# Splitting the last columns ahead of each RMS norm into two token halves in a two-layer trunk kernel

## What is computed

```python
def _rms(x, eps=NORM_EPS):
    xf = x.astype(jnp.float32)
    return (xf * lax.rsqrt(jnp.mean(xf * xf, axis=-1, keepdims=True) + eps)).astype(x.dtype)
def _modulate(h, shift, scale):
    return _rms(h) * (1.0 + scale) + shift
def _swiglu(h, w13, w2):
    a, b = jnp.split(h @ w13, 2, axis=-1)
    return (jax.nn.silu(a) * b) @ w2
for i in range(DEPTH):                       # DEPTH = 2, D = 1024, F = 2816
    h  = h  + 0.5 * ml[2] * _swiglu(_modulate(h,  ml[0], ml[1]), ffn1_w13[i], ffn1_w2[i])
    hc = hc + 0.5 * mc[2] * _swiglu(_modulate(hc, mc[0], mc[1]), ffn1_w13[i], ffn1_w2[i])
    a_l, a_c = _modulate(h, ml[3], ml[4]), _modulate(hc, mc[3], mc[4])
    o_l, o_c = mixer(a_l, a_c)               # i = 0: differential attention, i = 1: retention
    h = h + ml[5] * o_l
    h = h + 0.5 * ml[8] * _swiglu(_modulate(h, ml[6], ml[7]), ffn2_w13[i], ffn2_w2[i])
    # the context stream hc does the same in layer 0 only
return _rms(h) * final_norm_g
```

## The kernel before

| norm | phase ahead of it | phase behind it |
|---|---|---|
| n=1 | down, 16 chunks, 512 tokens | diff_qk, 512 tokens |
| n=2 | down of the attention, 4 chunks of 8, 512 tokens | up, 512 tokens |
| n=3 | down, 16 chunks, 512 tokens | up, 512 tokens |
| n=4 | down, 16 chunks, 512 tokens | ret_q, 256 tokens |
| n=5 | down of the retention, 8 chunks of 8, 256 tokens | up, 256 tokens |

## Time and profile before

### The profile page before, as it was taken

How to read it: one execution, slowest core, us unless ns; L and a number is a source line. 1 busy time by engine, 2 the same in 40 slices (tenths; PEclk the granted TensorE clock), 3 DMA queues, 4 the chain that set the end, 5 groups by cost and what they waited for, 6 DMA issues and landing times.

```text
span 2025.1 us, 28709 instructions
## 1 busy us (share of the span) xinstructions
PE 1951.5 (96%) x10376; PEld 1669.6 (82%) x10376; DVE 1155.0 (57%) x1834; ACT 661.6 (33%) x1020; POOL 203.4 (10%) x248
## 2 busy tenths in 40 slices
PE   8899999989988889999999899999989999999998
PEld 7688888878965678888888788888878998999998
DVE  3877773254368557787532777752352533656554
ACT  2323222232336332222222332222233422544443
POOL 1210100120001230100010310000120000011000
PEclk9799999989989889999999999999979999999999
DMA  7365652324210026656333355533224220455554
GB/s 280 119 204 187 195 173 88 99 85 161 84 63 1 1 68 211 198 188 198 122 92 106 134 198 192 194 119 101 86 86 154 95 83 22 132 181 165 175 166 138
DMA packets 80989, 270.61 MB, mean 134 GB/s; under 512 B 8992, under 2 KB 14368, under 8 KB 80800
## 3 DMA queue, kind: packets, MB, share of 16 engines
q1 hardware_dynamic: 62496, 202.69, 30.5%
q0 software_dynamic: 18432, 67.12, 10.3%
HBM read 268.72 MB, written 1.05 MB: 133 GB/s over the span
## 4 chain that ended last, share of the span: by engine, by line
PE 89%; DVE 7%; issue 2%; ACT 1%; POOL 1%; DMA 0%; DVEq 0%; POOLq 0%; SPq 0%; ACTq 0%
PE pt L1011 24%; PE pt L1012 24%; PE pt L1014 24%; PE pt L1186 2%; PE pt L1187 2%; PE pt L1185 2%; DVE tmp L790 2%; PE pt L1269 1%; DVE wl L643 1%; DVE tmp L784 1%; PE pt L1221 1%; PE pt L1202 1%; PE pt L1042 1%; DVE small L915 1%; PE pt L1259 1%
## 5 line engine op out<-in xcount | busy, mean ns | idle before, releaser
L643 DVE TENSOR_TENSOR wl<-raw,wh 128x1024 fp32r<-128x1024 f32 (+2 forms) x396 | 440.0, 1151 | 570.9 <-ACT wh L462 567.2
L1011 PE MATMUL pt<-xh,wh 128*128 128x512 f32 (+1 forms) x1824 | 662.2, 363 | 16.6 <-ACT xh L518 9.6
L1012 PE MATMUL pt<-xh,wl 128*128 128x512 f32 (+1 forms) x1824 | 659.8, 362 | 0.0
L1014 PE MATMUL pt<-xl,wh 128*128 128x512 f32 (+1 forms) x1824 | 651.8, 363 | 7.8 <-POOL xl L416 7.5
L462 ACT CAST wh<-raw 128x1024 fp32r<-128x1024 f32 (+2 forms) x396 | 365.5, 970 | 271.3 <-PE pt L1014 248.2
L1011 PEld LDWEIGHTS pt<-xh,wh 128*128 128x128 f32 x1824 | 351.5, 193 | 71.2 <-issue 11.0
L1014 PEld LDWEIGHTS pt<-xl,wh 128*128 128x128 f32 x1824 | 347.6, 192 | 65.5 <-POOL xl L416 15.8
L1012 PEld LDWEIGHTS pt<-xh,wl 128*128 128x128 f32 x1824 | 351.5, 193 | 50.6
L656 DVE CUSTOM_DVE_ANT_0 pt<-modw,raw 128x1024 f32<-128x1024 f32 x256 | 305.7, 1256 | 8.4 <-DMA modw<-in_mod_rows 8.3
L1011 PE MATMUL pt<-uh,wh 128*128 128x512 f32 (+1 forms) x704 | 257.5, 366 | 0.3 <-DVE wl L643 0.3
L1012 PE MATMUL pt<-uh,wl 128*128 128x512 f32 (+1 forms) x704 | 257.4, 366 | 0.0
(11 more groups left out here) (144 smaller groups left out, 1671.1 us busy)
## 6 DMA issues: line engine op xcount, KB each, us to landing
raw<-in_ffn_w SPq DMA_DIRECT2D x240, 512.0 KB, 4.0
modw<-in_mod_rows POOLq DMA_DIRECT2D x128, 512.0 KB, 4.0
raw<-in_ret_w_in SPq DMA_DIRECT2D x48, 512.0 KB, 4.3
raw<-in_diff_w_in SPq DMA_DIRECT2D x24, 512.0 KB, 4.2
raw<-in_ffn_w SPq DMA_DIRECT2D x32, 256.0 KB, 3.8
raw<-in_ret_w_out SPq DMA_DIRECT2D x16, 512.0 KB, 4.0
region<-in_mod_start SPq DMA_DIRECT2D x9, 512.0 KB, 8.6
raw<-in_ffn_w SPq DMA_DIRECT2D x32, 128.0 KB, 3.4
```

The source lines that it names most:

```text
L643: nc.vector.tensor_tensor(flat(wl[:, s, cut]), raw[:, raw_slot(late, s, p), 0:part_rows * CW], flat(wh[:, s, cut].bitcast(F32)), ALU.subtr ...
L1011: nc.tensor.matmul(bank, wh[:, s, k, cut], hi(k), start=a, stop=False)
L1012: nc.tensor.matmul(bank, wl[:, s, k, cut], hi(k), start=False, stop=False)
L1014: return nc.tensor.matmul(bank, wh[:, s, k, cut], lo(k), start=False, stop=b)
```

## The change

The last group of down (two output tiles) ahead of norms 1 to 5 is computed for the first half of the tokens and then for the second half, 256 tokens each (128 each at n=5). The first half takes all chunks of the group; the second takes the last two, which are still in wh and wl, and then the first two again (chunks 16 and 17, loaded once more; none at n=2 and n=5). The norm is made half by half: the first half's beside the passes of the second half, the second half's beside the first products of the next phase, which take their first pair of chunks by halves too (first_pair). Casts and rests of the chunks to come are put between tiles of the norm (split_at). The squares of the last two tiles are added on VectorE into ssq (fold), so each half needs two sum matmuls. Waits for weights are by piece (piece), waits for a PSUM bank by tile (claim). `small` gets 192 words, so that uh starts at byte 139136, a multiple of 128; oh and region move with it. The final norm is not split, but uses fold.

```diff
-        small = sb("small", [P, 176])
+        small = sb("small", [P, 192])
+        def chunks(ph):
+            return 4 * len(ph["rows"]) + ph["again"]       # again: 2 for four chunks a group, else 0
+        def last_group(ph):
+            nc_ = len(ph["rows"])
+            at = 3 * nc_
+            kept = range(max(nc_ - 2, 0), nc_)
+            return ([(at + e, e, 0) for e in range(nc_)] + [(at + e, e, 1) for e in kept]
+                    + [(4 * nc_ + e, e, 1) for e in range(ph["again"])])
+        def split_at(ph):
+            return {4: ({0: 16, 3: 17, 6: 18, DT: 19}, DT), 2: ({0: 8, 4: 9}, 2), 1: ({4: 5}, 2)}[len(ph["rows"])]
...
 VectorE, norm
+                    def normed_tile(half, k):
+                        i, cut = half * DT + k, slice(half * H, (half + 1) * H)
+                        if i >= 2:
+                            dve.wait_ge(x_hi_done, ph["xh"] + i - 1)
+                            dve.wait_ge(affine, ph["xh"] + i - 1)
+                        nc.vector.tensor_tensor(tmp[:, k % 2, cut], hT[:, k, cut], pt[:, BC + half, 0:H],
+                                                ALU.mult).then_inc(normed, 1)
+                    def statistics(half):
+                        norm_mean(ph["st"] + half, slice(half * H // P, (half + 1) * H // P), 4 + half)
+                        dve.wait_ge(bcast_ready, ph["st"] + half + 1)
+                    take_half(ph, 0)
+                    statistics(0)
+                    for k in range(DT):
+                        if k in splits:
+                            rest_chunk(ph["before"], splits[k])
+                        if k == other:
+                            take_half(ph, 1)
+                        if k == 0:
+                            normed_tile(0, 0)
+                        if k + 1 < DT:
+                            normed_tile(0, k + 1)
+                        affine_tile(0, k)
+                    if other == DT:
+                        take_half(ph, 1)
+                    if DT in splits:
+                        rest_chunk(ph["before"], splits[DT])
+                    statistics(1)
+                    normed_tile(1, 0)
+                    for k in range(DT):
+                        if k + 1 < DT:
+                            normed_tile(1, k + 1)
+                        affine_tile(1, k)
-                        rest(2 * q0 + 1, 1, late=late)
...
 ScalarE, norm
+                    half_squares(ph, 0)
+                    for k in range(DT):
+                        if k in splits:
+                            split_chunk(ph["before"], splits[k])
+                        if k == other:
+                            half_squares(ph, 1)
+                        half_tile(0, k)
...
 TensorE
+            def piece(chunk, k):
+                for p, row0 in enumerate((0, halves_of(DT)[0])):
+                    if k == row0:
+                        pe.wait_ge(lo_ready, 2 * chunk + p + 1)
+            def first_pair(ph, halves):
+                for half in halves:
+                    cut = slice(half * H, (half + 1) * H)
+                    for s in range(2):
+                        for k in range(DT):
+                            if half == 0:
+                                piece(2 * ph["q"] + s, k)
+                            pe.wait_ge(x_hi_done, norm["xh"] + half * DT + k + 1)
+                            ... (wh and wl by xh, both tiles; wait x_ready; wh by xl, both tiles)
+                            if half == 0 and s == 0 and k == DT // 2 - 1:
+                                half_sums(norm, 1)
+                            if half == 0 and s == 0 and k == DT - 1:
+                                half_spread(norm, 1)
...
 TensorE, down, behind the first three groups
+                        sums_at, spread_at = {4: ((0, 5), (1, 5)), 2: ((0, 7), (1, 7)), 1: ((0, 4), (1, 2))}[nc_]
+                        for i, (m, e, half) in enumerate(passes):
+                            for t in range(2):
+                                if first:
+                                    claim(half, s0[half] + 2 - half, t)
+                                for k in range(ph["rows"][e]):
+                                    if t == 0 and fresh:
+                                        piece(2 * q0 + m, k)
+                                    ... (three matmuls of T // 2 tokens)
+                                    if i == first_end + 1 and (t, k) == sums_at:
+                                        half_sums(norm, 0)
+                                    if i == first_end + 1 and (t, k) == spread_at:
+                                        half_spread(norm, 0)
+                            if spent:
+                                ins.then_inc(chunk_done, 1)
```

More of the change, by code:

```diff
@@ L110, in plan @@
             add("diff_attn", x=DH)
-            add("down", q=2, s=2, L=L, f=0, T=TOK, gate=5, half=1.0, rows=(8,))
+            down(L=L, f=0, T=TOK, rows=(8,), split=True)
         else:
@@ L455, in _, with split_chunk @@
         def _(act):
+            def split_chunk(ph, m):
+                chunk = 2 * ph["q"] + m
+                split(chunk // 2, chunk % 2, rows=chunk_rows(ph, m), late=chunk >= 2 * late_pair)
             def split(pair, s, rows=DT, late=False):
@@ L637, in _, with rest_chunk @@
         def _(dve):
+            def rest_chunk(ph, m):
+                chunk = 2 * ph["q"] + m
+                rest(chunk, chunk % 2, rows=chunk_rows(ph, m), late=chunk >= 2 * late_pair)
             def rest(chunk, s, rows=DT, late=False):
@@ L1004, in _, with products @@
         def _(pe):
-            def products(s, out_set, nk, hi, lo, T, start, stop, between=None, by_row=None):
+            def products(chunk, s, out_set, use, nk, hi, lo, T, start, stop, between=None, by_row=None):
                 def one(t, k, parts):
@@ L1023, in products @@
                     if stop:
[L1024 removed]
+                        a.then_inc(first_tile_done[out_set], 1)
                 else:
@@ new lines, in half_sums @@
+            def half_sums(norm, half, width=None):
+                H = width or norm["T"] // 2
+                pe.wait_ge(unit_step, UNIT_STEPS * (norm["unit"] - START_UNITS))
+                pe.wait_ge(sq_folded, norm["fold"] + 2 * (half + 1))
+                for b in range(H // P):
+                    ins = nc.tensor.matmul(pt[:, 4 + half, b:b + 1], ssq[:, half * H + b * P:half * H + (b + 1) * P], ones[:, 0:1],
+                                           start=True, stop=True)
+                ins.then_inc(sum_ready, 1)
@@ L1113, in norm_spread, with half_spread @@
+            def half_spread(norm, half, width=None):
+                H = width or norm["T"] // 2
+                pe.wait_ge(rstd_ready, norm["st"] + half + 1)
+                for b in range(H // P):
+                    at = half * H // P + b
+                    ins = nc.tensor.matmul(pt[:, BC + half, b * P:(b + 1) * P], rstd[:, at:at + 1].broadcast_to([P, P]), ident,
                                            start=True, stop=True)
@@ new lines, in _ @@
+                    for m in range((3 if ph["split"] else 4) * nc_):
+                        j, e = divmod(m, nc_)
+                        k0, rows_, g = first_row(ph, e), ph["rows"][e], j % 2
+                        by_row = None
+                        h_, l_ = (lambda k, k0=k0: hi(k0 + k)), (lambda k, k0=k0: lo(k0 + k))
+                        if m == 0 and not ph["f"]:
+                            by_row = (lambda k: pe.wait_ge(ready, upto + k + 1), lambda k: None)
+                        elif j == 0:
+                            pe.wait_ge(ready, upto + k0 + rows_)
+                        products(2 * q0 + m, m % 2, g, s0[g] + j // 2, rows_, h_, l_, T, e == 0, e == nc_ - 1, by_row=by_row)
```

483 lines of the change are left out of this document (267 added, 216 removed).

## The result

The changed kernel takes 2046.51 us (median of 4 runs, 2046.38 to 2051.52) beside 2025.31 us for the kernel before on the same chip (4 runs): a ratio of 1.0108, 95% interval 1.0091 to 1.0125. It is slower by 21 us, and outside my range (2023, 1997 to 2038).

What follows compares the result with a forecast made beforehand. TensorE was taken as the bound, busy 96% of the span, with 70.6 us of waits at five norms to win. Norm, address and final-norm terms summed to -3.3 us from 2026.3, giving 2023 us, range 1997 to 2038.

Steps and rivals of the forecast that it cites:

- Norms 1 to 3: Last down group through first pair behind each norm: changes of +0.6, -4.1 and +1.4 us forecast for n=1, 2 and 3.
- The table from S: Step times from S, start of the last down group, to the end of the first pair of chunks behind each norm.
- the rival that weights are not late: At n=1, 3 and 4 most of 11.4 us of stalls each would vanish: 1996 us, or some 1980; chance 0.25.
- Norm 4: Last down group through ret_q's first chunks: -1.1 us, with ret_q's second pair's first rest behind the second half's tiles, S+61.5.
- The address: Aligning u saves 7.0 us over 1188 matmuls at 512 tokens; at 256 tokens u costs +1.5 and o +2.2 us.
- Norm 5, the step that failed: 128-token matmuls at n=5 taken at 0.067 us each: 34.3 us for the stretch against 31.5 before, +2.8 us.
- The rule of the Trainium skill: A weight load of 128 columns takes 107 ns; by it n=5 costs +15.5 us, not +2.8, and the sum is 2035.
- one at 2036 us: Rival: the 384 matmuls of 128 tokens at n=5 are bound by their weight load, +12.7 us; chance 0.18.
- The clock rival: Stops of 2 to 3 us in split groups keep TensorE at 1.2 GHz, 1 to 3 us a norm: 2030 us; chance 0.07.
- The sum: All terms over the norms, the address of u and the final norm together: -3.3 us, giving 2023 us.

Runs made afterwards that it cites:

- experiment 5: Changed kernel with norm 5's down, norm and first pair whole at 256 tokens, loads of chunks 14 to 17 cut to 16 columns: 2004.58 us, ratio 0.9898.
- experiment 10: Matmuls alone, 72 per place of hi, lo and weights; 512 columns took 226.7 ns with hi and lo 0 or 256 bytes off, 228.9 at 64, 232.4 at 128.
- Experiment 2: The kernel before with one edit, small at 192 words so that u starts at a multiple of 128 bytes: 2018.51 us, ratio 0.9966.
- experiment 7: Changed kernel with only norm 5's first pair whole at 256 tokens, its last down group and tiles still in halves: 2030.82 us, ratio 1.0023.

## Why the prediction was wrong

*Norms 1 to 3, right.* The table from S gave 67.1, 42.4 and 67.1 us; measured 67.5, 42.2 and 67.4. Its waits in norm 1 were 2.5, 2.1, 0.8, 2.8, 2.2 and 1.0 us ahead of chunks 14, 15, 17, 18, the second sums and the second spread. Taken from start to start less one matmul they are 2.6, 1.7, 0.5, 2.9, 1.4 and 1.4. The cause of the first three is shown by experiment 5; the wait ahead of chunk 18 was left as it is there. So the rival that weights are not late is out, and the gain of the halves was zero by design: hidden norm out, open weight loads in.

*Norm 4, near.* I gave -1.1 us and it was 0.0. The wait for ret_q's second pair is there (4.4 us ahead of its first chunk at 1500.0, predicted 1501.8), and another 1.3 ahead of its second, which I had left out.

*The address, right in kind.* -7.0 us predicted, 1188 x 0.0066 = -7.8 measured, and +1.5 and +2.2 at 256 tokens came to 528 x 0.0014 = +0.7 and 288 x 0.0052 = +1.5. "Alignment" to 128 bytes was not the right name for it: in experiment 10 a place 128 bytes off is no faster than one 64 off. Experiment 2 shows it alone: 2018.5 of 2026.2 us.

*Norm 5, the step that failed.* "No row excludes either; I take 0.067." The 128-token matmul measured 0.111 us at the high clock, the bound that the earlier trace rows had given. 384 x 0.044 = 16.9 us. The rule of the Trainium skill that I weighed and set aside ("TensorE: Matmul & The Clock Gate", LDWEIGHTS: 107 ns for 128 columns, whatever the width of x) agrees with the 111 that 192 and 128 columns have in common. The row nearest in width said 0.111 and the rule said so too; the line through 512 and 256 tokens was an extrapolation past the point where another limit takes over.

The second part is the clock, which my sum for norm 5 put at nothing. The 144 matmuls at 0.2136 instead of 0.111 cost another 14.8 us. Together 31.7 over my 34.3, less some 2 that lay in the shadow of the paced tiles: 63.8. I had the two as rivals, one at 2036 us and one at 2030, and gave each its chance alone. The clock rival looked for stops in the split groups of 256 tokens. There the clock stayed at 1.00 at norms 1, 2 and 4 and fell once, at norm 3, for 3.4 us:
```profile
1077.03:1080.44 3.41, 3.41 (x19) 3.41 (x18) 0.00 (x0) 1.03 (x2) 0.00 (x0) 0.50 0.52 174
```
Norm 3 took 67.4 us even so, like norm 1. The rival did not look at the pair of norm 5, where the narrow matmuls make the stops matter. That dense narrow matmuls don't bring the clock back no row of before showed; but the range should have held both rivals at once, 2036 + 15 = 2051.

*The sum.* +1.0 - 4.5 + 1.6 + 0.0 + 32.2 - 7.8 + 0.7 + 1.5, and 2.3 us behind norm 5 while the clock recovers (117.5 us for 960 matmuls, 115.2 before), make +27.0; the spans differ by 19.7. The missing 7.3 us are in stretches that the diff doesn't touch: 4.7 ahead of the first u matmul (303.78 before, 299.06 after), 1.7 between norms 1 and 2, and 1.0 between norms 4 and 5. Part of the first is the clock. Before, after, and in experiment 7, whose code is the changed kernel's up to there and whose first u matmul comes at 303.2:
```profile
81.92:88.75 6.83, 5.05 (x12) 3.99 (x13) 6.83 (x11) 0.28 (x1) 0.53 (x1) 0.50 0.70 229
```
```profile
81.92:88.75 6.83, 6.83 (x32) 5.63 (x31) 6.74 (x12) 1.10 (x2) 1.06 (x2) 1.00 0.68 224
```
```profile
81.92:88.75 6.83, 6.11 (x14) 4.79 (x15) 6.83 (x11) 0.27 (x1) 0.53 (x1) 0.50 0.72 218
```
6.8 us at half the clock cost up to 3.4. The same code has it either way, so this is luck of the execution and no effect of the change. Each trace is one execution, and where the rest lies stays open.

## What to carry to other kernels

Before a stage is halved, read what each matmul has besides its columns: with a new weight load for each, 128 columns cost as much as 224 here (111 and 112 ns), so that a split from 256 to 128 nearly doubles the cost per token. Ask next what the halved pass no longer hides, here a load, cast and rest of 6.1 us behind passes of 3.6. And a place where TensorE is paced by another engine should be followed by wide matmuls, not by narrow ones.
